# A two-layer trunk on one core: buffers moved to multiples of 64 bytes, and another order of VectorE's and ScalarE's work in the first rounds of the feed-forward part

## Chip, cores and metric

The kernel runs on one core of a Trainium2 chip. The metric is the device time of one execution in microseconds (us); lower is better.

## The reference

A trunk of two layers over 512 tokens of width 1024, all in float32. Layer 0 mixes tokens by latent attention, layer 1 by a gated convolution of width 3. Behind each stands a SwiGLU of width 2816 (`D_FF`), and a final RMSNorm ends it. The change touches how the SwiGLU part is worked:

```python
def swiglu(h, w_gate, w_up, w_down):
    return (jax.nn.silu(h @ w_gate) * (h @ w_up)) @ w_down

for i in range(DEPTH):
    ...            # h = h + mixer(rms_norm(h, ...))
    h = h + swiglu(rms_norm(h, ffn_norm[i]), ffn_w_gate[i], ffn_w_up[i], ffn_w_down[i])
return rms_norm(h, final_norm)
```

## The kernel before

Activations lie transposed: features on the 128 partitions, the 512 tokens along the columns, in tiles of 128x512. Every float32 operand is held as two parts, a rounded one (`_hi`) and the rest (`_lo`), and every product is three matmuls: hi by hi, lo by hi, hi by lo (`product`, lines 453 to 455). Weights are the stationary operand.

Weights come as a stream of chunks of 128x2048 (1 MB) into two slots (s = 0, 1). SyncE loads `raw[s]` once `w_lo[s]` of the chunk before is made. ScalarE makes `w_hi[s]` (`split`, line 793) when the chunk is loaded and TensorE is done with the slot. VectorE makes `w_lo[s] = raw[s] - w_hi[s]` (`split`, line 1146). A chunk of eight k-tiles by two column tiles is 48 matmuls of 512 columns with w. Each engine runs its own list of instructions in the order in which it is written; semaphores tie the lists together.

The SwiGLU of a layer has 11 pairs of chunks (gate in slot 0, up in slot 1).

The first three, f = 0, 1, 2, are **plain rounds** (`PLAIN_ROUNDS = 3`). TensorE multiplies the unscaled input `f_hi`, `f_lo`; in round 0 it also sums squares (line 486). ScalarE takes the root (`rms`, line 798) and VectorE its reciprocal `rstd` (line 1178). In each round VectorE scales the gate by `rstd` (line 1183) once chunk 0 is done, ScalarE applies silu (line 1053), VectorE multiplies by `rstd` again (line 1500), and when chunk 1 is done it multiplies the up half in and so empties banks 2 and 3 (line 1508, into `inner`).

The other eight are **Winograd rounds**: each chunk is worked as 2x2 blocks with seven block products in place of eight, 84 matmuls of 256 columns: 48 with `w_hi`, `w_lo` and 36 with sums of weight blocks, `s_hi`, `s_lo`. They need two kinds of preparation:

- Sums of weight blocks: `forms(s)` on VectorE (lines 1440 to 1445), then `blocks_hi` and `sums_hi_of` on ScalarE (lines 1007 and 1011), then `forms_split` on VectorE (lines 1450 and 1452).
- Forms of the input, for four pairs of tiles k = 0 to 3: `x_forms` on VectorE (lines 1465 to 1475) writes seven forms into one of two buffers `x_form`, ScalarE rounds them (`x_hi_of`, line 1000), and VectorE takes the rest (`x_forms_split`, line 1481, `x_lo`). These four are made in plain rounds 0 and 1, two in each. The last plain round, f = 2, makes the first weight sums in their place.

The first Winograd round opens banks 0 to 3 and needs all four x_lo, `w_lo[0]` and the four banks emptied.

The down projections, the attention's and the convolution's matmuls with w have 512 columns, but for the values of a head (256 columns with w as the moving operand). The score matmuls have both operands in the arena.

**Addresses.** SBUF buffers are placed one behind the other, each at the next multiple of 32 bytes. `head` (75 + 4096 columns, 16,684 bytes) ends at byte 25,004 of a partition. The `arena`, in which `a`, `f`, `inner`, `x_hi`, `x_lo`, `s_hi`, `s_lo`, `x_form`, `oo`, `u` and `mid` share space, begins at byte 25,024, a multiple of 64. It is allocated with some bytes to spare, and `raw[0]` begins at 160,288 = 2504 x 64 + 32. So `raw`, `w_hi`, `w_lo`, `work`, `cos`, `rstd`, `acc`, `ident` and `ones` all begin 32 bytes past a multiple of 64.

Of the kernel before, what the change touches and what calls it, by code (L numbers as in the profile page):

```python
# [35 lines left out]
SEQ = 512  # L36
TOK = SEQ // P
D = 1024
KD = D // P
# [27 lines left out]
N_COLS = N_VEC + 5  # L67
# [13 lines left out]
PLAIN_ROUNDS = 3  # L81
# [17 lines left out]
ARENA = (38 + 2 * MID_TILES) * TILE_BYTES  # L99
# [67 lines left out]
def build(nc, x, head_in, positions, weights_in, out):  # L167
    with ExitStack() as ctx:
        def sb(name, cols, dt=F32):
            return ctx.enter_context(nc.sbuf_tensor(name, [P, cols], dt))  # L170
# [2 lines left out]
            return ctx.enter_context(nc.semaphore(name))  # L173


        head = sb("head", N_COLS + KD * SEQ)
        vec, xT = head[:, 0:N_COLS], head[:, N_COLS:N_COLS + KD * SEQ]
        arena_at = -(-nc.sbuf_base // 64) * 64
        sb("arena", (arena_at - nc.sbuf_base + ARENA + 64) // 4)
        assert nc.sbuf_base >= arena_at + ARENA  # L180

        def placed(name, at, cols, dt=F32R):

# [32 lines left out]
        def tile(t, m, n=SEQ):  # L216
            return t[:, m * SEQ:m * SEQ + n]
# [567 lines left out]
        def _(act):  # L785
            T = Tally()

            def split(s, n=SLOT):

                k = T.add(f"slot{s}")  # L790
                act.wait_ge(raw_loaded[s], (k - 1) * 16)
                act.wait_ge(chunk_done[s], k - 1)
                act.activation(w_hi[s][:, 0:n], raw[s][:, 0:n], ACT.Copy).then_inc(hi_split[s], 1)  # L793

            def rms(b, width):

                act.wait_ge(stat_summed, T.add("stat"))
                act.activation(bank[b][:, :], bank[b][:, :], ACT.Sqrt, bias=eps[:, 0:1], scale=1.0 / width).then_inc(rms_done, 1)
# [16 lines left out]
            def banks_used(uses):  # L815

                for b, n in uses.items():
                    T.add(b, n)
# [173 lines left out]
            def silu(m, b):  # L992

                act.wait_ge(drained[b], T.add(f"b{b}"))
                act.activation(tile(work, 3 + m), tile(work, 3 + m), ACT.Silu).then_inc(silu_done, 1)

            def x_hi_of(k):

                act.wait_ge(x_formed, T.add("x"))
                act.activation(x_hi[:, k * X_PAIR:(k + 1) * X_PAIR], x_form[k % 2][:, 0:X_PAIR], ACT.Copy).then_inc(x_hi_made, 1)  # L1000

            def blocks_hi(s):

                k = T.add(f"slot{s}")
                act.wait_ge(formed[s], T.add(f"formed{s}"))
                act.wait_ge(chunk_done[s], k - 1)
                act.activation(w_hi[s][:, :], raw[s][:, :], ACT.Copy).then_inc(hi_split[s], 1)  # L1007

            def sums_hi_of(s):

                act.activation(s_hi[s][:, :], sums, ACT.Copy).then_inc(sums_hi[s], 1)

            def copy(g, n):

                b = 4 * g + (n == 5)
                act.wait_ge(product_done[n], T.add(f"p{n}"))
                act.activation(copies[g][(1, 5, 6).index(n)], bank[b][:, 0:HT], ACT.Copy).then_inc(product_copied, 1)

            def copy_last(g):

                act.wait_ge(drained[4 * g + 2], T.add(f"b{4 * g + 2}"))
                act.wait_ge(chunk_done[g], T.now(f"slot{g}"))
                act.activation(copies[g][0], bank[4 * g][:, 0:HT], ACT.Copy).then_inc(drained[4 * g], 1)
                T.add(f"b{4 * g}")

            def inner_his(ms, ready):

                for m in ms:
                    if m >= 2 * PLAIN_ROUNDS:
                        act.wait_ge(inner_ready, ready + m + 1)  # L1030
                    take(tile(inner_hi, m), tile(inner, m))

            def gate():

                blocks_hi(1)
                copy(0, 1)
                sums_hi_of(1)
                copy(0, 5)
                copy(0, 6)
                copy_last(0)  # L1040

            def ffn(layer):
                for f in range(PLAIN_ROUNDS):
                    if f < PLAIN_ROUNDS - 1:
                        split(0)
                    else:
                        blocks_hi(0)
                        sums_hi_of(0)
                    if f == 0:
                        rms(4, D)  # L1050
                    act.wait_ge(drained[1], T.add("b1"))
                    for m in range(2):
                        act.activation(tile(work, 3 + m), tile(work, 3 + m), ACT.Silu).then_inc(silu_done, 1)
                    if f < PLAIN_ROUNDS - 1:
                        x_hi_of(2 * f)
                        split(1)
                        x_hi_of(2 * f + 1)
                banks_used(dict(b0=PLAIN_ROUNDS, b2=PLAIN_ROUNDS, b3=PLAIN_ROUNDS, b4=1))
                rest = KF // 2 - PLAIN_ROUNDS
                with T.loop(act, rest - 1, slot0=1, slot1=1, formed0=1, formed1=1, p1=2, p5=2, p6=2, b0=1, b1=1, b2=1, b3=1, b4=1, b6=1):  # L1060
                    gate()
                    blocks_hi(0)
                    copy(1, 1)
                    sums_hi_of(0)
                    copy(1, 5)
                    silu(0, 1)
                    silu(1, 3)
                    copy(1, 6)
                    copy_last(1)
                gate()  # L1070
                split(0)
                copy(1, 1)
                copy(1, 5)
                silu(0, 1)
                silu(1, 3)
                ready = layer * (KF - 2 * PLAIN_ROUNDS) - 2 * PLAIN_ROUNDS
                inner_his(range(2), ready)
                copy(1, 6)
                inner_his(range(2, 6), ready)
                copy_last(1)  # L1080
                inner_his(range(6, 12), ready)
                split(1)
                inner_his(range(12, KF), ready)
                banks_used({f"b{b}": rest for b in (5, 7)})
                residuals(DOWN_BANKS, 3, DOWN_AHEAD, layer == 1)
# [23 lines left out]
        def _(v):  # L1109
# [7 lines left out]
            def settle():  # L1117

                v.wait_ge(step, T.now("step"))
# [23 lines left out]
            def split(s, n=SLOT):  # L1143

                v.wait_ge(hi_split[s], T.add(f"slot{s}") - 1)
                v.tensor_tensor(w_lo[s][:, 0:n], raw[s][:, 0:n], w_hi[s][:, 0:n], ALU.subtract).then_inc(w_split[s], 1)  # L1146
# [34 lines left out]
            def scaled(m, b):  # L1181

                drain(b, v.tensor_tensor(tile(work, m), bank[b][:, :], rstd[:, :], ALU.mult))  # L1183
# [263 lines left out]
            def forms_split(s):  # L1447

                v.wait_ge(hi_split[s], T.add(f"slot{s}") - 1)
                v.tensor_tensor(w_lo[s][:, :], raw[s][:, :], w_hi[s][:, :], ALU.subtract).then_inc(w_split[s], 1)  # L1450
                v.wait_ge(sums_hi[s], T.add(f"sums{s}"))
                v.tensor_tensor(s_lo[s][:, :], sums, s_hi[s][:, :], ALU.subtract).then_inc(sums_split[s], 1)
# [24 lines left out]
            def x_forms_split(k):  # L1477

                v.wait_ge(x_hi_made, T.add("x"))
                cols = slice(k * X_PAIR, (k + 1) * X_PAIR)  # L1480
                v.tensor_tensor(x_lo[:, cols], x_form[k % 2][:, 0:X_PAIR], x_hi[:, cols], ALU.subtract).then_inc(x_split, 1)  # L1481

            def plain_round(f, name):

                done(0)
                all_ready()
                if f == 0:
                    inverse_rms(4)
                landed(2, 3)
                scaled(3, 0)  # L1490
                scaled(4, 1)
                if f < PLAIN_ROUNDS - 1:
                    split(0)
                    x_forms(name, 2 * f)
                else:
                    forms(0)
                    forms_split(0)
                for b in range(2):
                    v.wait_ge(silu_done, T.add("silu"))
                    do(v.tensor_tensor(tile(work, 3 + b), tile(work, 3 + b), rstd[:, :], ALU.mult))  # L1500
                settle()
                if f < PLAIN_ROUNDS - 1:
                    x_forms_split(2 * f)
                else:
                    forms(1)
                done(1)
                for b in range(2):
                    drain(2 + b, v.tensor_tensor(tile(inner, 2 * f + b), bank[2 + b][:, :], tile(work, 3 + b), ALU.mult))  # L1508
                if f < PLAIN_ROUNDS - 1:
                    split(1)  # L1510
                    x_forms(name, 2 * f + 1)
                    x_forms_split(2 * f + 1)

            def top_left(g, dst):

# [256 lines left out]
```

## Time and profile before

| | |
|---|---|
| time, median of 3 runs | 1122.6 us (1121.7 to 1122.76) |
| the profiled execution | 1120.92 us, its span 1119.1 us |
| granted TensorE clock, mean | 0.993 of full speed |
| TensorE busy with matmuls | 98% of the span |
| VectorE busy | 66% |
| ScalarE busy | 41% |

The span runs from the first to the last instruction of the profiled execution. A matmul's end is modelled, so that busy time is not time at peak; the distance between starts tells the pace. Idle time is put down to the instruction that was waited for last.

### The profile page before, as it was taken

The numbers are of one execution on the slowest core, as the hardware profiler recorded it, in microseconds if no ns is written. First come the engines' busy times: TensorE is split into PE (matmuls) and PEld (weight loads), VectorE is DVE, ScalarE is ACT, GpSimd is POOL, SyncE is SP. The second block draws the span as 40 slices with busy tenths as digits, with TensorE's granted clock in tenths as the row PEclk, the third lists the DMA queues.
The fourth block names the chain that finished last, engine by engine and source line by source line (L and its number), as shares of the span: only waits on it lengthen the run. The fifth ranks groups of instructions, "written<-read, shape, count | busy, mean of one in ns | idle before, by whom it ended". The sixth has DMA issues, their size and how long they took to land.

```text
span 1119.1 us, 16215 instructions
## 1 busy us (share of the span) xinstructions
PE 1096.3 (98%) x6208; PEld 952.7 (85%) x6208; DVE 735.3 (66%) x1013; ACT 453.9 (41%) x619; POOL 40.1 (4%) x22
## 2 busy tenths in 40 slices
PE   9999999999899999999999999999989999999997
PEld 7888888787899999888878888887879999988886
DVE  6667766588788887543346446667878888773332
ACT  6667772333445555322132212223344455551221
POOL 0232230000000000000000000000000000000000
PEclk9999999999899999999999999999989999999999
DMA  7211211222232222222222232222223332222211
GB/s 275 94 66 47 75 67 47 113 75 91 98 112 107 85 108 103 104 76 102 103 75 81 107 113 81 108 75 95 94 76 113 112 112 87 101 104 104 81 50 75
DMA packets 16963, 106.17 MB, mean 95 GB/s; under 512 B 1888, under 2 KB 2144, under 8 KB 6432
## 3 DMA queue, kind: packets, MB, share of 16 engines
q1 hardware_dynamic: 16848, 105.43, 26.1%
q8 instruction: 23, 0.38, 0.1%
q0 software_dynamic: 80, 0.26, 0.1%
q14 instruction: 12, 0.10, 0.0%
HBM read 103.59 MB, written 2.10 MB: 94 GB/s over the span
## 4 chain that ended last, share of the span: by engine, by line
PE 86%; DVE 9%; ACT 3%; issue 1%; DMA 1%; SPq 0%; DVEq 0%; ACTq 0%
PE bank L453 28%; PE bank L455 28%; PE bank L454 28%; DVE w_lo L1146 2%; ACT x_hi L1000 1%; PE bank L607 1%; PE bank L593 1%; DVE x_lo L1481 1%; DVE work L1183 1%; DVE inner L1508 1%; DVE rstd L1178 1%; DMA head<-head_in 1%; DVE x_form L1467 0%; DVE x_form L1465 0%; ACT w_hi L793 0%
## 5 line engine op out<-in xcount | busy, mean ns | idle before, releaser
L793 ACT ACTIVATE w_hi<-raw 128x2048 fp32r<-128x2048 f32 (+1 forms) x66 | 118.6, 1796 | 305.4 <-PE bank L455 305.3
L1146 DVE TENSOR_TENSOR w_lo<-raw,w_hi 128x2048 fp32r<-128x2048 f32 (+2 forms) x58 | 126.8, 2187 | 109.3 <-ACT w_hi L793 109.3
L453 PE MATMUL bank<-x_hi,w_hi 128*128 128x256 f32 x512 | 144.6, 282 | 12.0 <-DVE inner L1508 12.0
L454 PE MATMUL bank<-x_lo,w_hi 128*128 128x256 f32 x512 | 144.5, 282 | 0.0
L455 PE MATMUL bank<-x_hi,w_lo 128*128 128x256 f32 x512 | 144.4, 282 | 0.0
L455 PE MATMUL bank<-inner_hi,w_lo 128*128 128x512 f32 x352 | 139.6, 397 | 0.0
L454 PE MATMUL bank<-inner_lo,w_hi 128*128 128x512 f32 x352 | 139.6, 397 | 0.0
L453 PE MATMUL bank<-inner_hi,w_hi 128*128 128x512 f32 x352 | 139.6, 396 | 0.0
L453 PE MATMUL bank<-a_hi,w_hi 128*128 128x512 f32 x296 | 119.0, 402 | 1.6 <-DVE a_lo L1236 1.5
L455 PE MATMUL bank<-a_hi,w_lo 128*128 128x512 f32 x296 | 117.4, 397 | 0.0
L454 PE MATMUL bank<-a_lo,w_hi 128*128 128x512 f32 x296 | 117.3, 396 | 0.0
L453 PE MATMUL bank<-x_hi,s_hi 128*128 128x256 f32 x384 | 109.1, 284 | 0.0
L455 PE MATMUL bank<-x_hi,s_lo 128*128 128x256 f32 x384 | 108.7, 283 | 0.0
L454 PE MATMUL bank<-x_lo,s_hi 128*128 128x256 f32 x384 | 108.7, 283 | 0.0
L453 PEld LDWEIGHTS bank<-x_hi,w_hi 128*128 128x128 f32 x512 | 97.5, 191 | 12.8 <-DVE inner L1508 7.1
L455 PEld LDWEIGHTS bank<-x_hi,w_lo 128*128 128x128 f32 x512 | 97.4, 190 | 0.0
L454 PEld LDWEIGHTS bank<-x_lo,w_hi 128*128 128x128 f32 x512 | 97.4, 190 | 0.0
L1450 DVE TENSOR_TENSOR w_lo<-raw,w_hi 128x2048 fp32r<-128x2048 f32 x32 | 73.4, 2293 | 21.9 <-ACT w_hi L1007 20.3
L455 PEld LDWEIGHTS bank<-inner_hi,w_lo 128*128 128x128 f32 x352 | 66.3, 188 | 16.1
L453 PEld LDWEIGHTS bank<-inner_hi,w_hi 128*128 128x128 f32 x352 | 66.3, 188 | 16.1
L454 PEld LDWEIGHTS bank<-inner_lo,w_hi 128*128 128x128 f32 x352 | 66.3, 188 | 16.1
L453 PE MATMUL bank<-f_hi,w_hi 128*128 128x512 f32 x192 | 76.9, 401 | 0.0
(207 smaller groups left out, 2114.4 us busy)
## 6 DMA issues: line engine op xcount, KB each, us to landing
raw<-weights_in SPq DMA_DIRECT2D x82, 1024.0 KB, 4.8
raw<-weights_in SPq DMA_DIRECT2D x12, 768.0 KB, 4.2
raw<-weights_in SPq DMA_DIRECT2D x6, 512.0 KB, 3.8
work<-x SPq DMA_DIRECT2D x4, 512.0 KB, 6.1
head<-head_in SPq DMA_DIRECT2D x3, 512.0 KB, 8.2
out<-head SPq DMA_DIRECT2D x3, 512.0 KB, 3.4
out<-head SPq DMA_DIRECT2D x2, 256.0 KB, 4.0
head<-head_in SPq DMA_DIRECT2D x1, 293.5 KB, 3.3
```

The source lines that it names most:

```text
L453: pe.matmul(o, lhs[0], rhs[0], start=start, stop=False, skip_group_check=True)
L454: pe.matmul(o, lhs[0], rhs[1], start=False, stop=False, skip_group_check=True)
L455: return pe.matmul(o, lhs[1], rhs[0], start=False, stop=stop, skip_group_check=True)
L593: pe.matmul(o, qr, key, start=False, stop=False, skip_group_check=True)
L607: tr = pe.transpose(bank[b][:, j * P:(j + 1) * P], work[:, p0:p0 + P], ident[:, :])
L793: act.activation(w_hi[s][:, 0:n], raw[s][:, 0:n], ACT.Copy).then_inc(hi_split[s], 1)
L1000: act.activation(x_hi[:, k * X_PAIR:(k + 1) * X_PAIR], x_form[k % 2][:, 0:X_PAIR], ACT.Copy).then_inc(x_hi_made, 1)
L1146: v.tensor_tensor(w_lo[s][:, 0:n], raw[s][:, 0:n], w_hi[s][:, 0:n], ALU.subtract).then_inc(w_split[s], 1)
L1178: drain(b, v.reciprocal(rstd[:, :], bank[b][:, :]))
L1183: drain(b, v.tensor_tensor(tile(work, m), bank[b][:, :], rstd[:, :], ALU.mult))
L1450: v.tensor_tensor(w_lo[s][:, :], raw[s][:, :], w_hi[s][:, :], ALU.subtract).then_inc(w_split[s], 1)
L1481: v.tensor_tensor(x_lo[:, cols], x_form[k % 2][:, 0:X_PAIR], x_hi[:, cols], ALU.subtract).then_inc(x_split, 1)
```

## The change

Two things change.

1. `head` is rounded up to a multiple of 16 columns (16,704 bytes), the arena follows at the same byte 25,024 with no bytes to spare, and `raw[0]` and all that follows begin 96 bytes lower, at 160,192 = 2503 x 64. All their starts are then multiples of 64.
2. In the plain rounds:
   - VectorE takes the rest of an operand form (`x_forms_split`) one step later: that of pair 2f behind the products into `inner`, that of pair 2f + 1 in the next round behind the scalings. So the last of the four stands in round 2, ahead of `forms(0)`. In round 2 `forms_split(0)` moves behind the silu products.
   - ScalarE takes the root ahead of the first split, with a root of a single column ahead of it that loads its table. In round 2 silu stands ahead of `blocks_hi(0)` and `sums_hi_of(0)`.

```diff
-        head = sb("head", N_COLS + KD * SEQ)
+        head = sb("head", -(-(N_COLS + KD * SEQ) // 16) * 16)
         vec, xT = head[:, 0:N_COLS], head[:, N_COLS:N_COLS + KD * SEQ]
-        arena_at = -(-nc.sbuf_base // 64) * 64
-        sb("arena", (arena_at - nc.sbuf_base + ARENA + 64) // 4)
-        assert nc.sbuf_base >= arena_at + ARENA
+        arena_at = nc.sbuf_base
+        sb("arena", ARENA // 4)
+        assert arena_at % 64 == 0 and nc.sbuf_base == arena_at + ARENA
...
             def ffn(layer):
+                idle_sqrt()
+                rms(4, D)
                 for f in range(PLAIN_ROUNDS):
                     if f < PLAIN_ROUNDS - 1:
                         split(0)
-                    else:
-                        blocks_hi(0)
-                        sums_hi_of(0)
-                    if f == 0:
-                        rms(4, D)
                     act.wait_ge(drained[1], T.add("b1"))
                     for m in range(2):
                         act.activation(tile(work, 3 + m), tile(work, 3 + m), ACT.Silu).then_inc(silu_done, 1)
...
                         x_hi_of(2 * f)
                         split(1)
                         x_hi_of(2 * f + 1)
+                    else:
+                        blocks_hi(0)
+                        sums_hi_of(0)
...
                 scaled(3, 0)
                 scaled(4, 1)
+                if f > 0:
+                    x_forms_split(2 * f - 1)
                 if f < PLAIN_ROUNDS - 1:
                     split(0)
                     x_forms(name, 2 * f)
                 else:
                     forms(0)
-                    forms_split(0)
                 for b in range(2):
                     v.wait_ge(silu_done, T.add("silu"))
                     do(v.tensor_tensor(tile(work, 3 + b), tile(work, 3 + b), rstd[:, :], ALU.mult))
                 settle()
-                if f < PLAIN_ROUNDS - 1:
-                    x_forms_split(2 * f)
-                else:
+                if f == PLAIN_ROUNDS - 1:
+                    forms_split(0)
                     forms(1)
                 done(1)
                 for b in range(2):
                     drain(2 + b, v.tensor_tensor(tile(inner, 2 * f + b), bank[2 + b][:, :], tile(work, 3 + b), ALU.mult))
                 if f < PLAIN_ROUNDS - 1:
+                    x_forms_split(2 * f)
                     split(1)
                     x_forms(name, 2 * f + 1)
-                    x_forms_split(2 * f + 1)
```

## Rows read from the trace of the kernel before

**Rows 1.** Page, busy us (share of span) and instructions by engine

```profile
PE 1096.3 (98%) x6208; PEld 952.7 (85%) x6208; DVE 735.3 (66%) x1013; ACT 453.9 (41%) x619; POOL 40.1 (4%) x22
```

**Rows 2.** Waits over the span: total us, times, longest us

```profile
PE bank L453 <- DVE inner L1508: 12.0, 2, 6.7
...
DVE x_lo L1481 <- ACT x_hi L1000: 9.6, 8, 1.8
```

**Rows 3.** Timeline of TensorE, layer 0: start us, duration us, instruction

```profile
265.63 0.39 PE L455 MATMUL bank<-f_hi,w_lo 128*128 128x512 f32 x1
...
283.98 0.55 PE L453 MATMUL bank<-x_hi,w_hi 128*128 128x256 f32 x1 [6.71 <-DVE inner L1508]
```

**Rows 4.** Timeline of TensorE, layer 1

```profile
805.86 0.40 PE L455 MATMUL bank<-f_hi,w_lo 128*128 128x512 f32 x1
...
822.79 0.55 PE L453 MATMUL bank<-x_hi,w_hi 128*128 128x256 f32 x1 [5.28 <-DVE inner L1508]
```

**Rows 5.** Windows of 1 us: busy by engine, granted clock, DMA share, GB/s

```profile
280.00:281.00 1.00, 0.00 (x0) 0.00 (x0) 0.97 (x2) 0.00 (x0) 0.00 (x0) 0.56 1.00 426
...
286.00:287.00 1.00, 1.00 (x7) 1.00 (x6) 0.98 (x1) 0.08 (x1) 0.00 (x0) 0.52 0.00 0
...
826.00:827.00 1.00, 1.00 (x9) 1.00 (x9) 0.00 (x0) 1.00 (x2) 0.00 (x0) 0.87 0.48 57
```

**Rows 6.** Timeline of VectorE, end of round 1 and round 2, layer 0

```profile
266.83 2.03 DVE L1481 TENSOR_TENSOR x_lo<-x_form,x_hi 128x1792 fp32r<-128x1792 f32 x1 [1.77 <-ACT x_hi L1000]
268.77 1.28 DVE L1183 TENSOR_TENSOR work<-bank,rstd 128x512 f32<-128x512 f32 x2
...
274.69 2.29 DVE L1450 TENSOR_TENSOR w_lo<-raw,w_hi 128x2048 fp32r<-128x2048 f32 x1 [1.98 <-ACT w_hi L1007]
276.90 1.75 DVE L1452 TENSOR_TENSOR s_lo<-work,s_hi 128x1536 fp32r<-128x1536 f32 x1
278.56 1.29 DVE L1500 TENSOR_TENSOR work<-work,rstd 128x512 f32<-128x512 f32 x2
279.89 0.69 DVE L1440 TENSOR_TENSOR work<-raw 128x512 f32<-128x512 f32 x1
...
282.55 1.28 DVE L1508 TENSOR_TENSOR inner<-bank,work 128x512 f32<-128x512 f32 x2
```

**Rows 7.** The chain that ended last: start us, us, what

```profile
223.52 0.67 ACT bank L798
...
227.70 1.29 DVE work L1183 x2
...
807.57 1.28 DVE work L1183 x2
```

**Rows 8.** Timeline of TensorE in a Winograd round; 12 with w, 24 with s

```profile
308.12 0.28 PE L453 MATMUL bank<-x_hi,w_hi 128*128 128x256 f32 x1
...
309.53 0.29 PE L453 MATMUL bank<-x_hi,s_hi 128*128 128x256 f32 x1
...
312.40 0.28 PE L453 MATMUL bank<-x_hi,w_hi 128*128 128x256 f32 x1
```

**Rows 9.** Window of 100 us in the down projection of layer 0

```profile
450.00:550.00 100.00, 100.00 (x429) 80.41 (x428) 43.04 (x47) 25.59 (x27) 0.00 (x0) 1.00 0.27 97
```

**Rows 10.** Timeline of TensorE, scores of two heads, 512 columns

```profile
125.22 0.39 PE L454 MATMUL bank<-mid_lo,mid_hi 128*128 128x512 f32 x1
...
126.15 0.22 PE L595 MATMUL bank<-mid_hi 128*128 128x128 f32 x1
...
128.85 0.40 PE L454 MATMUL bank<-mid_lo,mid_hi 128*128 128x512 f32 x1
...
129.79 0.22 PE L595 MATMUL bank<-mid_hi 128*128 128x128 f32 x1
```

**Rows 11.** Groups by line and shape: count, busy us, mean ns, idle before

```profile
L455 PE MATMUL bank<-inner_hi,w_lo 128*128 128x512 f32 x352 | 139.6, 397 | 0.0
...
L455 PE MATMUL bank<-mid_hi,mid_lo 128*128 128x512 f32 x16 | 6.3, 393 | 0.0
```

## Prediction

> **What bounds the kernel now.** I read the page's busy times first: TensorE is busy for 98% of the span [rows 1]. So only two things can move the end: a stretch in which TensorE stands still, or the pace at which it issues. The waits come next: TensorE waits twice for "inner L1508", 12.0 us together, and hardly at all otherwise [rows 2]. Its timeline places both waits: each is the step from the last plain round into the first Winograd round, 6.71 us before 283.98 in layer 0 and 5.28 us before 822.79 in layer 1 [rows 3, 4]. The chain that ended last runs through VectorE and ScalarE in all plain rounds [rows 7].
>
> The clock belongs to this. In layer 0 the granted clock falls to half, 1.2 GHz, while TensorE stands (mean 0.56 within 280 to 281, so at about 280.1). It comes back only at about 286.96 (mean 0.52 in 286 to 287), 3.0 us after the restart; in layer 1 at about 826.26, 3.5 us after the restart [rows 5]. Work at half the clock takes up to twice as long, so beside its length each stall costs up to 1.5 and 1.7 us, 3.2 together.
>
> **Part 1: the order in the plain rounds.** What sets the restart at 283.98 is VectorE's work in round 2. It begins at 268.77 with the two scalings and ends with the products into inner, begun at 282.55 [rows 6]; TensorE starts 15.21 us after 268.77. TensorE had finished the chunk that this work waits for (chunk 0 of round 2) at 265.63 + 0.39 = 266.02 [rows 3]. VectorE came 2.75 us late. In layer 1 it began at 807.57 against 805.86 + 0.40 = 806.26, 1.31 us late [rows 4, 7].
>
> What is removed: VectorE stands still for ScalarE's x_hi once or twice per round, 9.6 us in 8 waits over both layers [rows 2], 1.77 of it right before the x_lo at 266.83 [rows 6]. That is 2.4 us per round, in two rounds per layer. With the subtraction one step later, x_hi is done by then: behind the first x_forms come the two silu products and the products into inner, behind the second the scalings. A round of VectorE, from scaling to scaling, takes (268.77 - 227.70) / 2 = 20.53 us in the trace [rows 6, 7]; without the waits 18.1. Two of them from the first scaling at 227.70 end at 263.9, before 266.02. So after the change VectorE waits for TensorE at the start of round 2 in both layers, and starts at about 266.07 and 806.31. It can't gain more than that there: 2.70 us and 1.26 us. The products into inner, which now stand ahead of x_lo, bring a new wait for TensorE's chunk 1. In round 1 the silu products end at about 253.4 and the chunk at 266.02 less its 11.25 us (48 matmuls of 0.2344, the step of [rows 9]), 254.8. Behind this wait stand the products (1.3 us), x_lo (1.94), the split (2.2) and x_forms (3.1): done at 263.3, so it is covered by 2.7 us. TensorE waits for that split at 266.02 and gets it at 260.2.
>
> What is added: the x_lo of pair 3 now stands inside round 2, ahead of forms(0), on the path: 1.94 us from start to start (266.83 to 268.77) [rows 6]. What is moved: the two silu products stood behind s_lo (278.56 to 279.89). They now run while ScalarE makes w_hi, in the wait of about 2 us ahead of the w_lo at 274.69; they need 1.3 us, so they fit. Then forms(1) begins right behind s_lo, at its end 276.90 + 1.75 = 278.65 plus 0.06 for the semaphore, where it began at 279.89: 1.18 us saved. The new length is 15.21 + 1.94 - 1.18 = 15.97 us. Restart in layer 0: 266.07 + 15.97 = 282.04, 1.94 us earlier; in layer 1: 822.28, 0.51 earlier. Together 2.4 us, of 12 us of stall.
>
> The root ahead of the split (and its table loaded while ScalarE is idle) brings the root from 223.52 to about 221.1 in layer 0, when TensorE's sum of squares is there, and the first scaling from 227.70 to about 225.3 [rows 7]. I cost it at nothing: round 2 already starts when TensorE allows. Its cover is the 2.1 us between 263.9 and 266.02; without the later subtractions it would have counted. Behind the root waits split(0), ready by about 223.7; VectorE asks for it after its scalings, at 226.6, and TensorE still later. In round 2 silu stands ahead of blocks_hi(0) on ScalarE: silu is over at 268.6, forms(0) at about 271.9, so it delays nothing. SP's loads wait for the same splits, which come earlier than now or at the same time.
>
> The clock can halve this gain. It has fallen by about 280.1, ahead of 282.0, so the restart is at the low level again. If it rises as long after the restart as now, the 2.4 us count whole; I take this. If it rises at the moment at which it rises now, the earlier time runs at half pace, and 1.2 us are left. If it came back at once, up to 3.2 us would be added.
>
> **Part 2: the addresses.** raw, w_hi, w_lo and what follows them stood 32 bytes past a multiple of 64; the arena stood on one already. VectorE shows no price for this. x_lo (1,792 elements, all in the arena) takes 2.03 us; w_lo (2,048, all outside) 2.29, s_lo (1,536, a mixed pair) 1.75 [rows 6]: from the latter two 1.05 ns an element, which gives 2.02 for x_lo. I cost VectorE and ScalarE at nothing, and the transfers too, since TensorE never waits for one.
>
> TensorE does show differences by where the stationary operand lies. In a Winograd round, moving x of the arena, 256 columns: 12 products with w (off by 32) from 308.12 to 309.53 are 0.1175 us apart, the next 24 with s (in the arena) to 312.40 are 0.1196 [rows 8]. If w paces like s once both lie alike, that is 2.1 ns on 1,536 products (32 chunks of 48): +3.2 us. With 512 columns the rows point the other way. In the down projections, w off by 32, 100 us hold 429 matmuls: 0.2342 apart [rows 9]. Score products with both operands in the arena stand 0.2325 apart over four (125.22 to 126.15) and 0.2350 in the other head (128.85 to 129.79) [rows 10]; by duration they are 393 ns against 397 [rows 11]. There are 2,952 products of 512 columns with w (3 x 352 of inner, the rest by the loops). At 0.2325 they give 1.7 ns each: -5.0 us; at 0.2350 they cost +2.4; by the durations -11.8. I take the middle one, -5.0, and for 256 columns the +3.2, since it has the same moving operand and the same rounds: -1.8 us. Bounds: -11.8 to +5.6.
>
> The Trainium skill speaks against this part. "SBUF — State Buffer", section "Who interferes with whom", gives TensorE two independent read ports, one for the moving operand and one for weight loads, and its "Specifications" name lines of 16 bytes, which both 32 and 64 respect. By these the addresses would change nothing. The trace differs a little: two paces, 0.1175 and 0.1196, under one shape [rows 8].
>
> **The sum.** -2.4 - 1.8 = -4.2 us. The profiled execution took 1120.9 us (span 1119.1), which gives 1116.7; the median lies 1.7 above it: 1122.6 - 4.2 = 1118.4.
>
> **Rivals.**
> (a) Addresses do nothing: the two paces of [rows 8] come from which products they are, not from bytes. Then 1122.6 - 2.4 = 1120.2. For it: the scores of one shape differ by head (0.2325, 0.2350) with all in the arena [rows 10]. Against it: within one head, too, w and the arena's operands keep different paces, 0.2342 and 0.2325. The page "SBUF — State Buffer" of the Trainium skill would have this case.
> (b) The 512-column gain comes without the 256-column loss, or reaches the durations' size: 1115.2, down to 1108.4.
> (c) Slower. Weight loads that lie in phase with the moving reads collide more in both shapes: 0.1196 and 0.2350 everywhere, +3.2 and +2.4, less the reorder's 2.4: 1125.8. It decides as soon as the two together pass 4.7 us. For it: s against w. Against it: the 0.2325 and the durations.
> (d) The reorder gives 1.2 us only, as the clock rises at the same moment, and addresses nothing: 1121.4.
>
> **How the numbers follow.** Forecast 0.38, (a) 0.27, (b) 0.15, (c) 0.10, (d) 0.10. A measurement tells 0.2%, 2.2 us, from no change: faster is below 1120.35. (a) sits on that edge and is split in halves: faster 0.38 + 0.13 + 0.15 = 0.66, same 0.14 + 0.10 = 0.24, slower 0.10. The range leaves out (c) and the deep end of (b): 1112.5 to 1124.0. The forecast's own range is 1116.5 to 1120.3.
>
> **What would show it.** TensorE's idle before its first product with x_hi is about 4.8 us in both layers, 9.5 together where it was 12.0. VectorE's scalings of round 2 begin within 0.1 us of TensorE's chunk 0 (266.1, 806.3); x_lo shows no wait for x_hi; w_lo of round 2 still waits 0.7 us for ScalarE. For the addresses: 12 products with w in a Winograd round are 0.1196 apart, and 100 us of down projection hold 432 matmuls instead of 429. The prediction is wrong if an x_lo still waits (rounds stay long), if the low clock lasts longer after the restart, or if the paces of TensorE stay as they are or go up in both shapes.

## The result

The changed kernel takes 1105.22 us in the median (1104.22 to 1106.18, 4 runs), the kernel before 1122.68 (1121.7 to 1123.09, 4 runs). The ratio is 0.9846, 95% interval 0.9829 to 0.9863: 17.5 us faster. The prediction was 4.2 us faster, 1118.4, with a range down to 1112.5. The direction was right; the size was off by a factor of four, and the time lies outside the range.

The profiled execution took 1105.14 us (span 1103.4), 15.8 under that of before. TensorE is busy for the same share of a shorter span, with the same 6,208 matmuls, so it issues faster [rows 1]:

```profile
PE 1081.8 (98%) x6208; PEld 956.0 (87%) x6208; DVE 734.9 (67%) x1013; ACT 454.2 (41%) x621; POOL 40.7 (4%) x22
```

The window in the down projection of layer 0 shows where. It held 429 matmuls in 100 us [rows 9] and now holds 443. From start to start that is 0.2267 us against 0.2343 (means of all distances between starts in the down projections). The first count is TensorE's, the second that of weight loads:

```profile
450.00:550.00 100.00, 100.00 (x443) 82.81 (x442) 41.83 (x45) 23.25 (x22) 0.00 (x0) 1.00 0.30 106
```

In a Winograd round the pace went the other way. TensorE's timeline, 12 products with s and then 12 with w, 1.44 us each, 0.1200 apart; w had 0.1175 [rows 8]:

```profile
292.12 0.28 PE L453 MATMUL bank<-x_hi,s_hi 128*128 128x256 f32 x1
...
293.56 0.28 PE L453 MATMUL bank<-x_hi,w_hi 128*128 128x256 f32 x1
...
295.00 0.28 PE L453 MATMUL bank<-x_hi,s_hi 128*128 128x256 f32 x1
```

The wait at the end of the plain rounds [rows 2, 3], from the waits and the timeline of TensorE:

```profile
PE bank L453 <- DVE inner L1508: 10.5, 2, 5.3
```
```profile
261.60 0.39 PE L455 MATMUL bank<-f_hi,w_lo 128*128 128x512 f32 x1
...
278.12 0.55 PE L453 MATMUL bank<-x_hi,w_hi 128*128 128x256 f32 x1 [5.25 <-DVE inner L1508]
```

VectorE's timeline of round 2 [rows 6]. There is no wait for x_hi ahead of x_lo, the silu products fill ScalarE's time for w_hi (0.85 us of it is left), and forms(1) follows s_lo:

```profile
262.03 1.29 DVE L1183 TENSOR_TENSOR work<-bank,rstd 128x512 f32<-128x512 f32 x2 [2.35 <-PE bank L455]
263.24 2.02 DVE L1481 TENSOR_TENSOR x_lo<-x_form,x_hi 128x1792 fp32r<-128x1792 f32 x1
...
267.83 1.28 DVE L1501 TENSOR_TENSOR work<-work,rstd 128x512 f32<-128x512 f32 x2
269.96 2.29 DVE L1450 TENSOR_TENSOR w_lo<-raw,w_hi 128x2048 fp32r<-128x2048 f32 x1 [0.85 <-ACT w_hi L1007]
272.17 1.75 DVE L1452 TENSOR_TENSOR s_lo<-work,s_hi 128x1536 fp32r<-128x1536 f32 x1
274.03 0.69 DVE L1440 TENSOR_TENSOR work<-raw 128x512 f32<-128x512 f32 x1
...
276.69 1.28 DVE L1508 TENSOR_TENSOR inner<-bank,work 128x512 f32<-128x512 f32 x2
```

The granted clock around both restarts [rows 5], windows of 1 us. In layer 0 it falls at about 276.8 and comes back at about 283.6, 5.5 us after the restart (3.0 before the change); in layer 1 it comes back at about 812.7, 4.0 us after the restart at 808.67 (3.5 before). The low stretch itself is as long as before, 6.8 us. It began 3.9 us ahead of the restart in layer 0 before the change and begins 1.3 us ahead of it now:

```profile
276.00:277.00 1.00, 0.00 (x0) 0.00 (x0) 0.96 (x3) 0.11 (x1) 0.00 (x0) 0.90 0.49 205
...
283.00:284.00 1.00, 1.00 (x8) 1.00 (x8) 1.00 (x1) 0.38 (x1) 0.00 (x0) 0.69 1.02 401
...
812.00:813.00 1.00, 1.00 (x7) 1.00 (x7) 0.00 (x0) 1.00 (x1) 0.00 (x0) 0.66 0.42 66
```

**The account.** 512 columns: (0.2343 - 0.2267) x 2,952 = -22.4 us. w with 256 columns: (0.1200 - 0.1174) x 1,536 = +4.0. Waits for inner: -1.5. Low clock: 3.0 us longer over both layers at half pace, +1.5. That is -18.4, where the span fell by 15.7. Of the rest, 2.0 us are lost ahead of the first plain round. The sum of squares behind its chunk 0 starts at 217.41 now and at 220.03 before, 2.6 us earlier, while the 600 or so products of 512 columns ahead of it should have given 4.6. TensorE's idle time up to there is the same, 4.0 us against 3.9. But in the attention part these products stand in short runs and don't reach 0.2267: neighbours are 0.2287 apart on average, against 0.2347 before. At that difference 600 of them give 3.6 us. The other 1.0 us, and some 0.7 us behind, are not accounted for.

TensorE's timeline of the changed kernel and of the kernel before:

```profile
217.41 1.02 PE L486 MATMUL bank<-acc,ones 128*128 128x512 f32 x2
```
```profile
220.03 1.02 PE L486 MATMUL bank<-acc,ones 128*128 128x512 f32 x2
```

### The profile page after: what moved, and what is told of

It reads as the page before. It is cut to its first block, busy times and chain, and to the rows that moved or that the text cites. A ratio compares the mean times of both kernels' runs of the same rounds, so it can differ in the third digit from the quotient of the medians.

```text
span 1103.4 us, 16219 instructions
## 1 busy us (share of the span) xinstructions
PE 1081.8 (98%) x6208; PEld 956.0 (87%) x6208; DVE 734.9 (67%) x1013; ACT 454.2 (41%) x621; POOL 40.7 (4%) x22
## 4 chain that ended last, share of the span: by engine, by line
PE 93%; DVE 4%; ACT 1%; DMA 1%; issue 0%; SPq 0%; DVEq 0%; ACTq 0%
PE bank L453 31%; PE bank L454 30%; PE bank L455 30%; PE bank L607 1%; PE bank L593 1%; DMA head<-head_in 1%; DVE w_lo L1450 0%; DVE x_lo L1481 0%; ACT w_hi L1007 0%; DVE rstd L1178 0%; DVE s_lo L1452 0%; DVE work L1183 0%; ACT w_hi L793 0%; DVE work L1442 0%; DVE work L1440 0%
## 5 line engine op out<-in xcount | busy, mean ns | idle before, releaser
L453 PE MATMUL bank<-x_hi,w_hi 128*128 128x256 f32 x512 | 146.3, 286 | 10.5 <-DVE inner L1508 10.5
L455 PE MATMUL bank<-x_hi,w_lo 128*128 128x256 f32 x512 | 145.9, 285 | 0.0
L453 PE MATMUL bank<-inner_hi,w_hi 128*128 128x512 f32 x352 | 137.0, 389 | 0.0
L454 PE MATMUL bank<-inner_lo,w_hi 128*128 128x512 f32 x352 | 137.0, 389 | 0.0
L455 PE MATMUL bank<-inner_hi,w_lo 128*128 128x512 f32 x352 | 136.9, 389 | 0.0
L455 PE MATMUL bank<-a_hi,w_lo 128*128 128x512 f32 x296 | 115.4, 390 | 0.0
L455 PE MATMUL bank<-x_hi,s_lo 128*128 128x256 f32 x384 | 109.4, 285 | 0.0
L455 PEld LDWEIGHTS bank<-x_hi,w_lo 128*128 128x128 f32 x512 | 99.4, 194 | 0.0
L455 PEld LDWEIGHTS bank<-inner_hi,w_lo 128*128 128x128 f32 x352 | 66.1, 188 | 13.7
L454 PEld LDWEIGHTS bank<-inner_lo,w_hi 128*128 128x128 f32 x352 | 66.1, 188 | 13.5
```

Source lines behind the costliest of these rows:

```text
L453: pe.matmul(o, lhs[0], rhs[0], start=start, stop=False, skip_group_check=True)
L454: pe.matmul(o, lhs[0], rhs[1], start=False, stop=False, skip_group_check=True)
L455: return pe.matmul(o, lhs[1], rhs[0], start=False, stop=stop, skip_group_check=True)
```

## The experiments

Each kernel differs from the changed kernel by the edit shown, if nothing else is said. Where only one time is given, it is one execution; the kernel before took 1121.2 to 1122.7 us (medians) on the same chips. A ratio is to that kernel, with its 95% interval, and need not equal the ratio of the medians. "Distance" is w's start minus the arena's, modulo 256 bytes. With w at 176,672 and the arena at 25,024 it was 96 before the change; it is 0 in the changed kernel (176,576).

### Order and addresses apart

**The order alone.** The allocation lines of before in the changed kernel.

```diff
-        head = sb("head", -(-(N_COLS + KD * SEQ) // 16) * 16)
+        head = sb("head", N_COLS + KD * SEQ)
...
+        arena_at = -(-nc.sbuf_base // 64) * 64
+        sb("arena", (arena_at - nc.sbuf_base + ARENA + 64) // 4)
```

> The new order with the old addresses (w and all that follows it 32 bytes past a multiple of 64). Theory A, addresses carry nearly the whole gain: the 512-column products keep the pace of before (429 matmuls in 100 us of down projection), the two waits for inner shrink from 12.0 to about 9.5 us together, and the time falls by 2 to 3 us, to about 1120. Theory B, the order carries it: 1106 to 1110.

1120.32 us (9 runs) against 1122.35, ratio 0.9972 (0.9962 to 0.9983): 2 us faster by the medians, 3 by the ratio. Its wait and its window:

```profile
PE bank L453 <- DVE inner L1508: 9.8, 2, 4.9
```
```profile
450.00:550.00 100.00, 100.00 (x429) 80.39 (x428) 42.70 (x46) 25.16 (x25) 0.00 (x0) 1.00 0.27 97
```

**The addresses alone.** The kernel before with the new allocation lines.

> The old order with the new addresses. Theory A: 443 matmuls in 100 us of down projection as in the changed kernel. The plain rounds have VectorE's chain of before, 20.5 us a round, so that the faster pace of their 512-column products (576 of the 2,952) only lengthens the waits for inner, to about 14 us together; time 1108 to 1111. Theory B: 1120.

1109.93 us (4 runs), ratio 0.9883 (0.9863 to 0.9904): 12 to 13 us faster. Its wait and window:

```profile
PE bank L453 <- DVE inner L1508: 15.5, 2, 8.5
```
```profile
450.00:550.00 100.00, 100.00 (x443) 82.84 (x442) 44.81 (x48) 26.23 (x27) 0.00 (x0) 1.00 0.28 97
```

Theory A holds: the addresses carry most of the gain. The two parts also help each other. With the old paces the order shortens the waits by 2.2 us (12.0 to 9.8), with the new ones by 5.0 (15.5 to 10.5): when TensorE finishes the plain chunks sooner, the old chain of VectorE holds it up for longer.

### Which address it is

**Only w_hi and w_lo on a multiple of 64.**

```diff
+        sb("pad0", 8)
         raw = [sb(f"raw{s}", SLOT) for s in range(2)]
+        sb("pad1", 8)
...
+        sb("pad2", 8)
         work = sb("work", 6 * SEQ)
```

> The changed kernel, but raw, work, cos, rstd, acc, ident and ones begin 32 bytes past a multiple of 64 again; only w_hi and w_lo stay on one. If the pace hangs on what TensorE itself reads: 443 matmuls in 100 us and about 1105 us, as in the changed kernel. If it hangs on what ScalarE and VectorE read and write beside it (raw, work): 429 matmuls and 1120 or more.

**Only w_hi and w_lo off by 32.** Both placed by hand, 32 bytes into a space that begins on a multiple of 64.

```diff
-        w_hi = [sb(f"w_hi{s}", SLOT, F32R) for s in range(2)]
+        sb("w_space", 4 * SLOT + 16)
+        w_hi = [nc.alloc_sbuf_tensor_at(f"w_hi{s}", [P, SLOT], F32R, offset=w_at + s * SLOT * 4 + 32) for s in range(2)]
```

> The complement: the changed kernel with w_hi and w_lo alone 32 bytes past a multiple of 64. If TensorE's own read of the weights sets the pace: 429 matmuls in 100 us, w's products of 256 columns at 0.1175 us instead of 0.1200, about 1121 us. If ScalarE's and VectorE's other buffers set it: 443 matmuls and about 1105 us.

Both were slow, 1117.53 and 1118.29 us, and both windows hold 430:

```profile
450.00:550.00 100.00, 100.00 (x430) 80.57 (x429) 42.34 (x45) 23.49 (x22) 0.00 (x0) 1.00 0.28 97
```
```profile
450.00:550.00 100.00, 100.00 (x430) 80.49 (x430) 43.09 (x45) 24.24 (x23) 0.00 (x0) 1.00 0.26 97
```

Neither of two complementary edits keeps the gain, which fits no theory as it stood. The pads of the first had moved w by 64 bytes: a multiple of 64, but at distance 64. From this came theory D: the distance counts.

**Everything 32 bytes higher, the distance kept.**

```diff
-        head = sb("head", -(-(N_COLS + KD * SEQ) // 16) * 16)
+        head = sb("head", -(-(N_COLS + KD * SEQ) // 16) * 16 + 8)
```

> The changed kernel with arena, raw, w and all that follows moved up by 32 bytes together: no large buffer begins at a multiple of 64 any more, but stationary and moving operands still lie a multiple of 512 bytes apart. So far the fast pace (443 matmuls in 100 us of down projection) was seen only where w and the arena both begin 64 bytes past a multiple of 128; w 64 bytes off that gave 430, 32 below it 429, 32 above it 430. Theory D, the distance between the two operands counts: 443 matmuls, about 1105 us. Theory M, multiples of 64 count: 429 to 430 matmuls, 1117 us or more.

**w first, at the same distance; raw, work and the rest off by 32.**

```diff
+        w_hi = [sb(f"w_hi{s}", SLOT, F32R) for s in range(2)]
+        w_lo = [sb(f"w_lo{s}", SLOT, F32R) for s in range(2)]
+        sb("pad0", 8)
         raw = [sb(f"raw{s}", SLOT) for s in range(2)]
```

> The changed kernel with w_hi and w_lo first behind the arena, 160,192 and up, at the same distance from it modulo 512 bytes as in the changed kernel, and raw, work, cos, rstd, acc, ident and ones behind them 32 bytes past a multiple of 64. It repeats the question of the run in which only w was on 64 without moving w by 64 bytes. Theory D and theory M with TensorE's operands alone: 443 matmuls in 100 us and about 1105 us. If ScalarE's and VectorE's buffers count as well: fewer.

1104.60 and 1104.57 us, as fast as the changed kernel, with no large buffer of the first on a multiple of 64:

```profile
450.00:550.00 100.00, 100.00 (x443) 82.81 (x442) 41.41 (x45) 22.81 (x21) 0.00 (x0) 1.00 0.30 108
```
```profile
450.00:550.00 100.00, 100.00 (x443) 82.78 (x442) 41.55 (x45) 22.99 (x21) 0.00 (x0) 1.00 0.30 107
```

Multiples of 64 are not the cause, and neither are the buffers that only ScalarE and VectorE touch. What is left is how far TensorE's stationary operand lies from its moving one; moving x in place of w, further down, bears it out.

**w at other distances.** One pad ahead of w_hi, of 32, 64, 48, 40 and 56 columns (128, 256, 192, 160 and 224 bytes):

```diff
         raw = [sb(f"raw{s}", SLOT) for s in range(2)]
+        sb("pad0", 32)
         w_hi = [sb(f"w_hi{s}", SLOT, F32R) for s in range(2)]
```

> The changed kernel with w_hi, w_lo and what follows 128 bytes higher: still a multiple of 64, distance from the arena 128 modulo 512 in place of 0. Theory D with a period of 128 bytes, and theory M: 443 matmuls in 100 us, about 1105 us. Theory D with a longer period: 430, about 1117 us.

> The changed kernel with w_hi, w_lo and what follows 256 bytes higher: distance 256 modulo 512. Theory D with a period of 128 or 256 bytes, and theory M: 443 matmuls in 100 us, about 1105 us. Theory D with a period of 512: 430, about 1117 us.

> The changed kernel with w_hi, w_lo and what follows 192 bytes higher, a distance of 192 modulo 256 that no run has had. Theory D: 0 alone is fast, so 429 to 432 matmuls in 100 us of down projection and about 1117 us. If multiples of 64 were enough in some places: 443 and 1105.

> The changed kernel with w_hi, w_lo and what follows 160 bytes higher. It fills the table of distances (so far for 512 columns: 0 fast, 32 to 128 slow, 192 between; for 256 columns: 192 fast, 0 slowest). Theory D as a smooth curve with its best 256-column distance near 192: w's 256-column products between 0.1135 and 0.1188, and 432 to 438 matmuls in 100 us of down projection.

> The changed kernel with w_hi, w_lo and what follows 224 bytes higher, 32 short of 256. Smooth curve: w's 256-column products between 0.1135 and 0.1200, and 438 to 443 matmuls in 100 us. If multiples of 64 are a condition of their own: 429 to 432 matmuls, as at 32 and 96.

Windows of the down projection at 128, 256, 192, 160 and 224:

```profile
450.00:550.00 100.00, 100.00 (x432) 81.09 (x431) 43.23 (x45) 24.36 (x24) 0.00 (x0) 1.00 0.27 97
```
```profile
450.00:550.00 100.00, 100.00 (x443) 82.81 (x442) 43.69 (x46) 25.10 (x25) 0.00 (x0) 1.00 0.28 99
```
```profile
450.00:550.00 100.00, 100.00 (x438) 82.05 (x438) 36.33 (x36) 20.12 (x16) 0.00 (x0) 1.00 0.27 97
```
```profile
450.00:550.00 100.00, 100.00 (x430) 80.43 (x429) 43.69 (x48) 26.00 (x27) 0.00 (x0) 1.00 0.27 97
```
```profile
450.00:550.00 100.00, 100.00 (x431) 80.30 (x430) 42.22 (x45) 23.27 (x22) 0.00 (x0) 1.00 0.27 97
```

All distances together. The pace is the mean distance between starts; the x_hi, x_lo products with w have 256 columns, those of the down projections 512. s stayed at distance 0 in all of them and at 0.1195 to 0.1200. The comparison rests on the paces: most rows are one execution, and the times also hold what the clock did in it (at 32, 64, 128, 192 and 224 the low stretch of layer 0 was 3.4 us long, in the others 6.8).

| distance | in 100 us | 512 columns, us | 256 columns with w, us | time, us |
|---|---|---|---|---|
| 0 (changed kernel) | 443 | 0.2267 | 0.1200 | 1105.2 |
| 0 (256 higher) | 443 | 0.2267 | 0.1200 | 1106.95 |
| 32 | 430 | 0.2333 | 0.1184 | 1118.29 |
| 64 | 430 | 0.2333 | 0.1179 | 1117.53 |
| 96 (order alone) | 429 | 0.2343 | 0.1174 | 1120.3 |
| 128 | 432 | 0.2324 | 0.1188 | 1117.26 |
| 160 | 430 | 0.2333 | 0.1196 | 1121.88 |
| 192 | 438 | 0.2289 | 0.1133 | 1098.91 |
| 224 | 431 | 0.2333 | 0.1170 | 1116.81 |

256 bytes higher changes no pace, so over the distances tried it counts modulo 256. The run at 192 went against the expectation, by 18 us. Its 512-column products are between fast and slow, and its 256-column products with w are the fastest of all, as TensorE's timeline shows: 33 starts in 3.74 us, 0.1133 apart.

```profile
306.72 0.28 PE L456 MATMUL bank<-x_hi,w_lo 128*128 128x256 f32 x1
...
310.46 0.28 PE L456 MATMUL bank<-x_hi,w_lo 128*128 128x256 f32 x1
```

So each width has its own best distance, 0 for 512 columns and 192 for 256, and the curve is not smooth.

### Towards a faster kernel

**x 160 bytes higher**, which puts w and s 96 from x and leaves the 512-column operands at 0.

```diff
-FORMS_AT = 12 * TILE_BYTES
-INNER_AT = 40 * TILE_BYTES
+FORMS_AT = 12 * TILE_BYTES + 160
+INNER_AT = 40 * TILE_BYTES + 256
```

> The changed kernel with the moving forms x_hi and x_lo alone 160 bytes higher in the arena (inner 256 higher to make room), so that w and s both lie 96 modulo 256 from them, as w did before the change; w and the 512-column operands stay at 0. Theory D (the distance of the two operands modulo 256): all 2,688 products of a Winograd round run at 0.1174 to 0.1178 us, w and s alike, where both have 0.1200 now; the 512-column products keep 443 in 100 us; time down by 6 to 7 us, to about 1098.5. If s's pace hangs on which products they are: s stays at 0.1200 and the gain is 4 us or less.

1099.14 us (4 runs, 1097.39 to 1101.97), ratio to the kernel before 0.9797 (0.9776 to 0.9818). Both w and s run at 0.1173, as w did at 96 with w moved. The 24 products with s in TensorE's timeline:

```profile
304.24 0.28 PE L453 MATMUL bank<-x_hi,s_hi 128*128 128x256 f32 x1
...
307.06 0.28 PE L453 MATMUL bank<-x_hi,w_hi 128*128 128x256 f32 x1
```

s follows the distance as w does, so its pace had nothing to do with which products it makes.

**The products into inner ahead of forms(1)** in the last plain round.

```diff
                 if f == PLAIN_ROUNDS - 1:
                     forms_split(0)
-                    forms(1)
                 done(1)
                 for b in range(2):
                     drain(2 + b, v.tensor_tensor(tile(inner, 2 * f + b), bank[2 + b][:, :], tile(work, 3 + b), ALU.mult))
+                if f == PLAIN_ROUNDS - 1:
+                    forms(1)
```

> The changed kernel with the products into inner of the last plain round ahead of forms(1) on VectorE. If the wait at the end of the plain rounds hangs on VectorE's chain up to these products: the two waits for inner shrink by forms(1), 2.7 us each, from 10.5 to about 5.1 together, and the time by 5.4 us or, if the clock then stays up, by up to 8, to 1097 to 1100. If TensorE was held by something else (a split, x_lo): no change.

1097.13 us (4 runs), ratio 0.9771 (0.9755 to 0.9788), 8.1 us under the changed kernel. The waits fall to 4.8 us together, and the clock doesn't fall here any more: after the restart at 275.27 the products are 0.12 apart at once.

```profile
PE bank L453 <- DVE inner L1507: 4.8, 2, 2.4
```
```profile
275.27 0.36 PE L453 MATMUL bank<-x_hi,w_hi 128*128 128x256 f32 x1 [2.40 <-DVE inner L1507]
275.46 0.28 PE L454 MATMUL bank<-x_lo,w_hi 128*128 128x256 f32 x1
275.58 0.28 PE L455 MATMUL bank<-x_hi,w_lo 128*128 128x256 f32 x1
```

5.7 us are the waits. The clock should have given more than the other 2.4: in the changed kernel 24 and 17 distances behind the restarts are 0.213 us, where 0.120 would have saved 3.8 us. But forms(1) now comes later, so ScalarE starts the w_hi made from it 1.0 us later (277.89), and the copy behind that (line 1017), which frees a bank, holds TensorE up. The first product with s starts 0.59 us behind the product ahead of it, and three more are late by 0.1 us each, 0.8 us in each layer:

```profile
280.12 0.39 PE L453 MATMUL bank<-x_hi,s_hi 128*128 128x256 f32 x1 [0.31 <-ACT work L1017]
```

**Both.**

> Both: x 160 bytes higher and the products into inner ahead of forms(1). The two act at different places, so the gains add: 12 to 15 us under the changed kernel, 1090 to 1093.5. If the second takes away what hid the first: less than 10.

1093.46 us (4 runs), ratio 0.9735 (0.9717 to 0.9754): 11.8 under the changed kernel, where the two alone give 6.1 and 8.1. At the same distance of 96, w and s run at 0.1187 here and at 0.1173 without the second edit, 3.8 us over 2,688 products, which is enough for the 2.4 that are missing. The clock also fell again at one of the two waits, at about 800.0 in layer 1, for 3.4 us.

**x 64 bytes higher**, so that w and s lie 192 from it (`FORMS_AT = 12 * TILE_BYTES + 64`), and the same with the products into inner first.

> The changed kernel with x_hi and x_lo 64 bytes higher in the arena (inner 256 higher), so that w and s lie 192 modulo 256 from them, while w and the 512-column operands stay at 0. Theory D with a best distance for each width (0 for 512 columns, 192 for 256): all 2,688 products of the Winograd rounds run at about 0.1135 us, s too, and 443 matmuls stay in 100 us of down projection; 6.5 ns on each, 17 us under the changed kernel, about 1088. Rival: VectorE and ScalarE can't feed rounds of 9.5 us in place of 10.1 (they were busy for 111 and 65 of 130 us), and half of it is lost: 1095 to 1098. If only w can pace so: 1095 too, with s at 0.1200.

> The same with the products into inner ahead of forms(1) in the last plain round. If the gains add: about 8 us less than with the distance alone, about 1080. If the clock or the feed of the Winograd rounds takes part of it, as the pair at distance 96 lost 3 us (0.1187 in place of 0.1173): 1083 to 1086.

1099.18 us (5 runs, 1093.70 to 1099.61), ratio 0.9795 (0.9780 to 0.9810), and 1091.74 us (5 runs, 1091.41 to 1092.00), ratio 0.9729 (0.9715 to 0.9742): 6 and 13.5 us under the changed kernel, where 17 and 25 were expected. The profiled execution of the first has two paces, 0.1178 in layer 0 and 0.1133 in layer 1, with the same instructions at the same addresses. It took 1093.70 us; the other four took 1098.68 to 1099.61, some 5.5 us longer, and 1,344 products at 0.1178 in place of 0.1133 are 6.0. By this estimate they had the slower pace in both layers, as the profiled execution of the second kernel has. Windows in the Winograd rounds of layer 0 (130 us) and layer 1 (100 us), first of the kernel with x moved, then of that with inner first as well:

```profile
300.00:430.00 130.00, 130.00 (x1107) 130.00 (x1106) 111.52 (x142) 65.67 (x92) 0.00 (x0) 1.00 0.30 105
850.00:950.00 100.00, 100.00 (x884) 100.00 (x884) 89.20 (x114) 51.56 (x73) 0.00 (x0) 1.00 0.31 113
```
```profile
300.00:430.00 130.00, 130.00 (x1107) 130.00 (x1106) 111.03 (x141) 66.38 (x95) 0.00 (x0) 1.00 0.29 105
850.00:950.00 100.00, 100.00 (x851) 100.00 (x851) 84.70 (x108) 51.55 (x72) 0.00 (x0) 1.00 0.29 105
```

The rival, that VectorE can't feed faster rounds, falls with the first: in layer 1, at 884 in 100 us, TensorE was never idle. The loss is in the pace itself, which has more than one steady value at one distance.

**s 64 bytes higher as well**: w 192 from x, s 0 from it.

```diff
-SUMS_AT = [0, 6 * TILE_BYTES]
+SUMS_AT = [64, 6 * TILE_BYTES + 64]
```

> The changed kernel with x 64 bytes higher and s 64 bytes higher as well, so that w lies 192 modulo 256 from x and s lies 0 from it; 512-column operands stay at 0. At distance 192 for w and s alike one layer ran at 0.1178 us and the other at 0.1133 in the same execution, while with s at 0 both layers had w at 0.1133. Theory E, each distance has more than one steady rhythm and a stretch of s at 0 in every chunk brings w back to the fast one: w at 0.1133 and s at 0.1200 in both layers, 6.7 ns on 1,536 products, 10 us under the changed kernel, about 1095, and the single times close together. Theory D alone can't tell s's place from w's pace: w at 0.1133 or 0.1178 by chance, times spread over 5 us as before.

> The same with the products into inner ahead of forms(1) in the last plain round. Theory E: the gains add, 10 and 8 us, about 1087, 4 to 5 us under the same kernel with s at distance 192 too (1091.7), with w at 0.1133 in both layers. Without theory E: w at 0.1178, and with s at 0.1200 slower than that kernel, about 1094.

1097.45 us (4 runs, 1094.91 to 1097.89), ratio 0.9770 (0.9755 to 0.9785), and 1088.49 us (5 runs, 1086.63 to 1089.10), ratio 0.9693 (0.9680 to 0.9706). In both layers of both kernels w runs at 0.1133 and s at 0.1200. The second is the fastest of all, 33.4 us under the kernel before and 16.7 under the changed one. Its windows:

```profile
300.00:430.00 130.00, 130.00 (x1121) 130.00 (x1120) 112.77 (x143) 67.97 (x97) 0.00 (x0) 1.00 0.30 105
850.00:950.00 100.00, 100.00 (x863) 100.00 (x862) 85.47 (x107) 52.62 (x75) 0.00 (x0) 1.00 0.29 105
```

With the run at distance 192 for w alone, w paced at 0.1133 in six of six layers where s lay at 0, and in one of four where s lay at 192 too. That speaks for theory E, that the stretch of s brings w back to the fast rhythm. Six against four layers is no proof of the mechanism. The first time is 2.5 us above what theory E expected, but not for the pace: in its profiled execution the first plain round starts at 208.45, 1.9 us later than in the changed kernel, behind a stretch of 3.4 us from about 12.6 in which the clock was low; the changed kernel has none there:

```profile
13.00:14.00 1.00, 1.00 (x3) 0.78 (x3) 1.00 (x2) 1.00 (x2) 0.00 (x0) 0.50 0.80 320
```

## Why the prediction was wrong, point by point

**What bounds the kernel**: right. TensorE's pace and its two waits for inner are all that moved.

**The new order**: right, nearly to the tenth. The scalings of round 2 start at 262.03, when TensorE's chunk 0 ends (261.60 + 0.39), in place of 2.75 us late. From there to the restart pass 16.09 us; 15.97 were predicted. The order alone gave 2 to 3 us (1.9 to 4.3 by its interval) for the 2.4 predicted, and its waits were 9.8 us for 9.5. The root moved ahead shows as costed: VectorE waits 2.35 us for TensorE ahead of round 2, so there was nothing to gain by it there; it was not tried alone.

**The low clock**: the length assumed was wrong. It lasted 5.5 and 4.0 us after the restarts in place of the 3.0 and 3.5 that I carried over. The low stretches are 6.8 us long in both kernels; what moved is where in the wait they begin. Between the two profiled executions this took back some 1.5 us. The run with the products into inner first got 2.6 us beyond its shorter waits, the clock's gain less its new delay.

**The addresses, 512 columns**: here the prediction failed. The term was mis-sized: -5.0 us predicted, with -11.8 as its bound, and -22.4 by the measured paces. Each down projection is 4.0 us shorter from first to last start, each set of plain rounds 2.1, as 7.6 ns on each product give; only the attention part gave less. The step that failed is the one that took the scores as stand-in, "Score products with both operands in the arena stand 0.2325 apart over four". Those rows do lie at distance 0, and they are the same in the changed kernel: four distances in 0.93 us, 0.2325, as in [rows 10]:

```profile
151.67 0.39 PE L454 MATMUL bank<-mid_lo,mid_hi 128*128 128x512 f32 x1
...
152.60 0.22 PE L595 MATMUL bank<-mid_hi 128*128 128x128 f32 x1
```

A run of four between matmuls of other widths does not show the pace that hundreds alike settle into, 0.2267. The changed kernel shows this with w itself. These eight products with w, at distance 0 as well, stand in a short run of the attention part, and their seven distances are 0.2314 on average:

```profile
168.31 0.40 PE L454 MATMUL bank<-oo_lo,w_hi 128*128 128x512 f32 x1
...
169.93 0.39 PE L455 MATMUL bank<-oo_hi,w_lo 128*128 128x512 f32 x1
```

Over all runs of 512-column matmuls in the changed kernel the second distance is 0.233 us on average, the eighth 0.228, and from the eleventh on it is 0.227. In the kernel before it is 0.233 to 0.235 at every one of these places. So the two kernels are alike at the start of a run and part only further on. By duration the scores are 393 ns in both kernels, while the L455 products of the down projections went from 397 to 389. No row of the trace of before had a long run of 512 columns at distance 0, so neither end of my bounds was one.

The experiments put the cause beyond doubt in one respect: at distance 0, modulo 256, the pace is 0.2267 in all twelve kernels traced, wherever the buffers lie; at six of the seven other distances it is 0.2324 to 0.2343.

**The addresses, 256 columns**: right. +3.2 was predicted from s, +4.0 came. This stand-in worked since s had the same moving operand and long runs, and was at distance 0 already.

**The reason given**: half right. The prediction spoke of both "alike" and "in phase", and took the multiple of 64 as the change. That multiple does nothing: everything 32 bytes off it is as fast. The change hit distance 0 because the bytes to spare around the arena went.

**The rivals**: (a), that addresses do nothing, is refuted: with w moved by 32 bytes, the same matmuls run at 0.2333 in place of 0.2267. The Trainium skill gives TensorE two independent read ports in "SBUF — State Buffer", "Who interferes with whom". No run here tests the ports; but to conclude from them that the operands' addresses change nothing, as this rival does, was wrong. (b), the 512-column gain beyond my figure, names the right direction, but its 256-column half was wrong and its depth, 1108.4, was still short. (c) is refuted by the 512 columns, (d) by the order's 1.9 us or more and by the addresses' 12.

## What to carry to other kernels

Where TensorE is the bound and streams of like matmuls are long, measure the distance between starts, and try the distance of the stationary and the moving buffer modulo 256 bytes as a parameter of its own: one pad of a few columns made the changed kernel anything from 6 us faster to 17 us slower, each width has its own best value, and an aligned start by itself was worth nothing. A bound for a steady stream must come from a steady stream; a handful of matmuls between others is no bound. And of the work on a chain that TensorE waits for, put first what empties its banks: moving one call behind these products was worth 8 us, 5.7 of them the wait and the rest the clock, which stayed up in that kernel.

## What the runs showed of the hardware that was not expected

- In long runs the pace of 256-column float32r products is 0.1200 us at distance 0 and 0.1133 at 192; that of 512-column ones 0.2267 at 0 and 0.2343 at 96. At distance 192 the three products of a triple had paces of their own in the down projections: 0.2258 with inner_hi and w_hi, 0.2292 with inner_lo and w_hi, 0.2317 with inner_hi and w_lo.
- The pace at one distance can have more than one steady value: 0.1133 and 0.1178 at 192, 0.1173 and 0.1187 at 96. What picks it stays open; w at 192 had the faster pace in all six layers in which s lay at 0, which is not shown to be the cause. Why the distance acts at all, and why modulo 256, stays open too: no run looked inside.
- A wait of 5.3 us brought the clock down to its lower level, 1.2 GHz, in both layers of the changed kernel, and it stayed there for 5.5 and 4.0 us of work. Around the eight waits of 2.4 us (two in each of the four kernels with the products into inner first) it stayed at the upper level, 2.4 GHz, five times. In layer 1 of three of them it fell, 0.6 and 0.9 us behind the restart and, in the fastest kernel, 0.2 us ahead of it, and was low for 3.4 us. So a wait of 2.4 us does not keep the clock up by itself. The fastest kernel around its restart at 798.04:

```profile
798.00:799.00 1.00, 0.96 (x4) 0.99 (x5) 0.96 (x2) 0.00 (x0) 0.00 (x0) 0.50 1.04 442
```
